# Sums of fetched activations formed on GpSimd, and two output banks copied by ScalarE, in a seven-product fp32 decoder trunk

## The reference

```python
for layer in range(2):
    mixer = fox_mixer if layer == 0 else retention_mixer
    h = h + mixer(rmsnorm(h, norm), ...)
    h = h + square(relu(rmsnorm(h, mlp_norm) @ w_up)) @ w_down    # 2048 -> 8192 -> 2048
return rmsnorm(h, final_norm)
```

## Time and profile before

| | us |
|---|---|
| median of 3 runs | 2564.88 (2563.68 to 2568.09) |
| the profiled execution | 2560.97 |
| its span, first to last instruction | 2559.2 |
| TensorE busy | 2489.9 (97%) |
| VectorE busy | 1962.1 (77%) |
| ScalarE busy | 1446.4 (57%) |
| GpSimd busy | 165.1 (6%) |

### The profile page before, as it was taken

One profiled execution on the slowest core, in us unless ns is written; L12 is line 12 of the kernel. 1 busy time (PEld: TensorE's weight loads), 2 busy tenths in 40 slices (PEclk: granted clock), 3 DMA queues, 4 the chain that ended last, 5 costly groups with the idle time before them and its releaser, 6 DMA issues. The chain is left out here.

```text
span 2559.2 us, 29454 instructions
## 1 busy us (share of the span) xinstructions
PE 2489.9 (97%) x11035; PEld 2045.9 (80%) x11035; DVE 1962.1 (77%) x2007; ACT 1446.4 (57%) x1694; POOL 165.1 (6%) x284
## 2 busy tenths in 40 slices
PE   9999999999999999989999999999999999999998
PEld 8888888788788787768888888888777887878876
DVE  6454556888787888867778867778888888788877
ACT  7454544656555656545556446556565556565654
POOL 0000000000100001101111001101100010010010
PEclk9999999999999999999999999999999999999999
DMA  8454556575757565756665666666576666657574
GB/s 311 150 176 149 172 174 226 189 256 193 231 182 259 187 244 196 248 168 206 214 220 184 233 187 216 199 201 224 206 247 217 221 213 202 228 194 258 179 237 163
DMA packets 133940, 534.79 MB, mean 209 GB/s; under 512 B 17200, under 2 KB 17456, under 8 KB 133424
## 3 DMA queue, kind: packets, MB, share of 16 engines
q1 hardware_dynamic: 115776, 476.65, 54.1%
q0 software_dynamic: 17888, 56.12, 7.3%
q10 hardware_dynamic: 144, 0.26, 0.0%
HBM read 506.74 MB, written 26.21 MB: 208 GB/s over the span
## 5 line engine op out<-in xcount | busy, mean ns | idle before, releaser
L1530 ACT ACTIVATE w_hi<-work 128x1024 fp32r<-128x1024 f32 (+2 forms) x847 | 960.6, 1154 | 718.8 <-DMA work<-in_w_wide 172.3
L2152 DVE TENSOR_TENSOR w_lo<-work,w_hi 128x1024 fp32r<-128x1024 f32 (+2 forms) x847 | 1117.0, 1348 | 323.8 <-ACT w_hi L1530 320.5
L1047 PE MATMUL acc<-w_hi,xT_hi 128*128 128x512 f32 x811 | 319.0, 393 | 7.9 <-DVE xT_lo L2218 3.9
L1049 PE MATMUL acc<-w_hi,xT_lo 128*128 128x512 f32 x811 | 317.4, 391 | 0.0
L1048 PE MATMUL acc<-w_lo,xT_hi 128*128 128x512 f32 x811 | 317.2, 391 | 0.0
L1047 PE MATMUL sc<-w_hi,xT_hi 128*128 128x512 f32 x676 | 264.1, 391 | 0.0
L1049 PE MATMUL sc<-w_hi,xT_lo 128*128 128x512 f32 x676 | 263.2, 389 | 0.0
L1048 PE MATMUL sc<-w_lo,xT_hi 128*128 128x512 f32 x676 | 263.0, 389 | 0.0
L1047 PE MATMUL acc<-w_hi,aT_hi 128*128 128x512 f32 x584 | 232.1, 397 | 11.2 <-DVE aT_lo L2218 5.5
L1915 DVE TENSOR_TENSOR w_lo<-work,w_hi 128x1024 fp32r<-128x1024 f32 x127 | 151.7, 1223 | 103.2 <-ACT w_hi L1322 100.9
L1048 PE MATMUL acc<-w_lo,aT_hi 128*128 128x512 f32 x584 | 229.3, 393 | 0.0
(11 more groups left out here) (321 smaller groups left out, 3887.6 us busy)
## 6 DMA issues: line engine op xcount, KB each, us to landing
work<-in_w_stream SPq DMA_DIRECT2D x400, 512.0 KB, 4.6
work<-in_w_wide SPq DMA_DIRECT2D x212, 768.0 KB, 6.6
work<-in_w_wide SPq DMA_DIRECT2D x178, 512.0 KB, 5.9
park<-stage POOLq DMA_DIRECT2D x38, 512.0 KB, 4.1
evac<-park POOLq DMA_DIRECT2D x152, 128.0 KB, 4.2
qk_park<-evac POOLq DMA_DIRECT2D x8, 512.0 KB, 6.0
work<-qk_park POOLq DMA_DIRECT2D x32, 128.0 KB, 5.4
h<-in_x SPq DMA_DIRECT2D x2, 1024.0 KB, 8.7
```

The costliest lines, as they stand in the source:

```text
L1047: pe.matmul(bank[:, :], x_hi, w_hi[:, c], start=start, stop=False, skip_group_check=True)
L1049: return pe.matmul(bank[:, :], x_lo, w_hi[:, c], start=False, stop=stop, skip_group_check=True)
L1530: ins = act.activation(w_hi[:, ring_cols(place, n)], src[:, first * NB:(first + n) * NB], ACT.Copy)
L2152: ins = dve.tensor_tensor(w_lo[:, c], src[:, first * NB:(first + n) * NB], w_hi[:, c].bitcast(F32), ALU.subtract)
```

## The change

1. VectorE's `wide_sums` and `turned_sums` are gone. GpSimd forms the sums in `turn`, behind the fetch of the turn that they need, with four `tensor_tensor` instructions and waits on its own semaphores; then it goes on to the next turn. There are 19 such groups: turns 0 and 1 of each of the eight chunks (256 and 128 columns), one group of 256 ahead of retention, and one of 256 and one of 128 ahead of the second MLP. The first MLP's very first sums are formed in another way, as before.
2. After a down pair that isn't followed by a norm (i = 3, 4, 7, 8, 11, 12 in each MLP) ScalarE copies banks e and w into the two `tr` banks (`copy_out`), ahead of `seed_u`, and VectorE adds the copies to `h` later, after `lo(7)` and `lo(8)` (`add_copy`).
3. After an up pair `seed_u` stands ahead of the square of the third relu.
4. In pair 15 ScalarE's first two squares of `h` move behind `hi(8)`, and VectorE's last `turn_lo` behind the add and the gain of its own banks. In retention's last output pair the second turn's `turn_hi` and `turn_lo` stand ahead of tile 16 instead of behind tile 17, and the split of the sums stands one tile earlier.

```diff
+            def turned_sums(n, count, first, j, sign):
+                w = width_of_sum(count)
...
+                pool.wait_ge(fetched, GRID * 16 * (n + 1))
+                wait(pool, s_lo, count - 1)
+                small_step(pool.tensor_tensor(s[S1], a21, a22, ALU.subtract))
+                if sign > 0:
+                    small_step(pool.tensor_tensor(s[S2], a11, s[S1], ALU.subtract))
+                else:
+                    small_step(pool.tensor_tensor(s[S2], s[S1], a11, ALU.subtract))
+                pool.tensor_tensor(s[S3], a11, a21, ALU.subtract)
+                pool.tensor_tensor(s[S4], a12, s[S2], ALU.subtract if sign > 0 else ALU.add).then_inc(s_made, 1)
+                pool.wait_ge(s_made, parts_of_sums(count - 1) + (2 if first else 1))
...
+                for m in range(2):
+                    chunk, quad = divmod(n - UPS_AT[m], QUADS)
+                    if 0 <= chunk < SUPER and quad < 2:
+                        turned_sums(n, UNITS[mlp_unit(m, 4 * chunk + 2)].sums, quad * 2 * P, 2 - quad, -1)
...
+            def copy_out(tok, done, bank, out, count, n):
+                act.wait_ge(done, count)
+                act.wait_ge(turned, n)
+                wait(act, copy_added[tok], T(f"copy{tok}"))
+                act.activation(tr[tok], bank[:, :], ACT.Copy).then_inc(out, 1)
+                T.up(f"copy{tok}")
...
@@ ScalarE, wide_pair
                 if was_up:
                     relu(0, e_done, sc[0], e_out, done, turn + 1)
                     relu(1, w_done, sc[1], w_out, done, turn + 1)
+                if copies:
+                    turns = UPS_AT[m] + (i + 1) // 4 * QUADS
+                    copy_out(0, e_done, sc[0], e_out, done, turns)
+                    copy_out(1, w_done, sc[1], w_out, done, turns)
+                seed_u(u, RET_HEADS * m)
+                if was_up:
                     relu_squared(0, e_out, done)
-                seed_u(u, RET_HEADS * m)
...
+            def add_copy(tok, quad, out, count):
+                dve.wait_ge(out, count)
+                dve.scalar_tensor_tensor(h_quad(tok, quad), tr[tok], inv_ms[:, tok:tok + 1], h_quad(tok, quad),
+                                         ALU.mult, ALU.add).then_inc(copy_added[tok], 1)
...
@@ VectorE, wide_pair
-                if not was_up:
+                if was_normed:
                     add_bank(0, p_quad + 1, sc[0], e_done, e_out, done, scaled=not by_pe)
...
                 lo(u, 7)
+                if copies:
+                    add_copy(0, p_quad + 1, e_out, done)
                 lo(u, 8)
+                if copies:
+                    add_copy(1, p_quad + 1, w_out, done)
                 if turn is not None and not late_norm:
-                    if new_sums:
-                        wide_sums(turn, 0)
                     turn_lo(turn, *dst, p_quad)
```

More of the change, by code:

```diff
@@ L152, in parts_of_sums, with width_of_sum @@
     return sum(1 if X_SUMS_OF_RET <= n < X_SUMS_OF_MLP else 2 for n in range(1, count + 1))
+def width_of_sum(count):
+    return (KT_SEVEN if X_SUMS_OF_RET <= count < X_SUMS_OF_MLP else KT_WIDE) // 2 * P
 def tiles_of(u):
@@ L599, in build_trunk @@
         full_out = sem("full_out")
+        copy_added = pair("copy_added")
+        sum_step = sem("sum_step")
         x_done, z_done, e_done, w_done = (sem(f"{n}_done") for n in ("x_bank", "z_bank", "e_bank", "w_bank"))
@@ L755, in _, with small_step @@
             load_gain(0)
+            def small_step(ins):
+                ins.then_inc(sum_step, 1)
+                small_steps[0] += 1
+                pool.wait_ge(sum_step, small_steps[0])
+            small_steps = [0]
+            def turned_sums(n, count, first, j, sign):
+                w = width_of_sum(count)
+                s = [mlp_sums[:, k * w + first:k * w + first + j * P].rearrange("p (j a r) -> p j a r", j=j, a=GRID)
+                     for k in range(4)]
+                (a11, a12), (a21, a22) = ([fetched_tiles[:, t, at:at + j] for at in (0, j)] for t in range(TOKS))
+                pool.wait_ge(fetched, GRID * 16 * (n + 1))
[8 more added lines that the diff above has]
+                pool.wait_ge(s_made, parts_of_sums(count - 1) + (2 if first else 1))
             def turn(n):
@@ L1307, in _ @@
         def _(act):
-            T = Tally("block", "tr0", "tr1", "squared", "group", "ret_head", "norm", "p5")
+            T = Tally("block", "tr0", "tr1", "squared", "group", "ret_head", "norm", "p5", "copy0", "copy1")
             def split(first, last, block0=False):
@@ L1705, in wo_pair @@
                     batch_hi(1, aT_hi, QUADS - 1)
-                for t in range(13, 18):
+                for t in range(13, 16):
                     hi(u, t)
@@ L1722, in wide_pair @@
                 new_sums = UNITS[u + 1].sums if i % 4 == 1 else 0
+                copies = not was_up and not was_normed
                 if by_pe:
@@ L1755, in wide_pair @@
                 hi(u, 8)
+                if late_norm:
+                    square_of_h(0, p_quad, x_out, done)
+                    square_of_h(1, p_quad, z_out, done)
                 if was_normed:
@@ L2411, in wo_pair @@
                 fold(1, quad + 1, g_sum, False)
+                if was_normed:
+                    turn_lo(MLP_NORM_AT + 1, xT_hi, xT_lo, 1)
                 lo(u, 16)
@@ L2414, in wo_pair @@
                 if was_normed:
-                    wide_sums(MLP_NORM_AT + 1, 1)
-                    turn_lo(MLP_NORM_AT + 1, xT_hi, xT_lo, 1)
+                    s_low(X_SUMS_OF_MLP)
                 add_bank(0, quad, acc[0], x_done, x_out, done + 1, scaled=False)
@@ L2503, in wide_pair @@
                     s_low(new_sums)
-                if turn is not None and late_norm:
-                    turn_lo(turn + 1, *dst, p_quad + 1)
                 if not up and u not in LATE:
@@ L2511, in wide_pair @@
                         wait_gain(dve, 1)
+                        dve.wait_ge(turned, turn + 2)
                         gained_after(0, quad, x_out, done + 1)
+                if turn is not None and late_norm:
+                    turn_lo(turn + 1, *dst, p_quad + 1)
             def rotated(hd, tok):
```

38 lines of the change are left out of this document (9 added, 29 removed).

## The result

| | before | after |
|---|---|---|
| median of 4 runs, us | 2564.28 (2562.52 to 2568.09) | 2589.77 (2585.92 to 2594.06) |
| the profiled execution, us | 2560.97 | 2589.35 |
| its span, us | 2559.2 | 2587.3 |
| mean granted TensorE clock | 0.990 | 0.985 |

The account below looks back on a forecast made before the run. One chain per chunk, from turn 1's transposes through DRAM to the seed, was taken to bound TensorE. 2.0 + 1.6 - 0.5 = +3.1 us a chunk, +24.8 for eight, -2.6 for copies: +22.2, so 2587 us; range 2557 to 2604.

Parts of the forecast that it names:

- Sums of turn 1: Behind turn 1's landing: GpSimd's four sums of 128 columns start `s_high` 3.95 instead of 2.35 us after it, +1.6 a chunk.
- the first rival: Sums stay beside the chain: those of turn 1 end within 2.35 us of the landing; -6.6 us, 2558 us; 18%.
- Sums of turn 0: Mid-pair: GpSimd's four sums of 256 columns stop VectorE 3.2 us, transposes of turn 1 up to 2.8 late; +2.0 a chunk.
- the last sentence: Of turn 0's term: a later write falls behind part of the weight loads, so only 2.0 of the 2.8 us pass on.
- The rival in which the DMA swallows the delay: Turn 1 lands when it did despite turn 0's late sums; only 1.6 - 0.5 a chunk remain, +6, 2571 us; 15%.
- Seed ahead of the square: Chain's end in each chunk: the seed starts at the square's earlier place, -0.5 us; the square, wanted much later, is covered.
- The copies: After down pairs: VectorE loses two adds ahead of `seed_w`, -2.6 us in all; ScalarE's two copies cost 0.
- The norms: Pair 15 and retention's last pair: both ends wait for TensorE itself, so 0, bounds -1.6 and +3.2 us.
- GpSimd is the one that waits: VectorE keeps GpSimd out: turn 0's sums run from `seed_w` on, S3 and S4 after `lo(last)`; +22, also 2587 us; 10%.
- Gains and losses cancel: Rival: sums of turn 0 free, those of turn 1 half a microsecond late; 2560 to 2570 us; 12%.
- What should show it: Seed waits beyond 30 us or new up-pair waits; VectorE 0.5 to 0.8 us longer; landing to `s_high` over 3; `seed_w` waits gone.

Follow-up runs that it names:

- sums_alone: Kernel before with only edit 1, all 19 groups of sums on GpSimd instead of VectorE: 2601.7 us, ratio 1.0139.
- sums_back: Changed kernel with all sums back on VectorE at their old places; copies, seed ahead of the square and moved turns stay: 2566.45 us, 1.0004 to before.
- turn0_alone: Kernel before with only the sums of 256 columns (turn 0 of each chunk, first turns of the norms) on GpSimd: 2585.65 us, ratio 1.0093.
- seed_down: Kernel before with the seed ahead of the square only in each chunk's first down pair: 2560.3 us, ratio 0.9983.
- turn1_alone: Kernel before with only the sums of 128 columns (turn 1) on GpSimd: 2580.22 us, ratio 1.0064.
- seed_up: Kernel before with the seed ahead of the square only in each chunk's second up pair: 2573.83 us, ratio 1.0035.

## Why the prediction was right, and where it wasn't

The time (2589.8 against 2587) and the direction came out as forecast, and by the mechanism forecast: GpSimd's sums on the chain of turn 1, shown by sums_alone and sums_back. But errors of opposite sign stand inside, and that the total is so near is in part luck.

- **Sums of turn 1, +1.6 a chunk.** 1.77, in all eight. The single pieces were off: 0.46 us for a sum where I took 0.55, and 0.08 us from one to the next where I took 0.5 from the earlier trace rows. Undisturbed, four would be over about 2.1 us after the landing, ahead of the 2.35 us that the first rival sets, and this term would have been 0. What decided was the taking of turns, S3 behind `turn_lo` and S4 behind `w_lo`. The forecast let S4 follow S3 without a gap; a `w_lo` between them was its bad end, priced +2.7. That order came, with shorter pieces, and that the two errors meet near 1.6 is luck. The trace shows that the stop works in both directions, which the prediction had no row for: the 1.51 us are GpSimd standing behind VectorE. The Trainium skill (SBUF — State Buffer, "Who interferes with whom") has the later one wait for a whole instruction, and these rows agree: VectorE, back to back, lets one GpSimd instruction in between two of its own.
- **Sums of turn 0, +2.0 of 2.8.** Two errors that cancel in part. The four sums held VectorE up by 2.2 us and not 3.2, so the delay ahead of the write was 1.8 us and not the 2.8 it could be. And the last sentence failed: the transfer swallowed none of it, its mean became 1.0 longer. The term read from the traces is +2.8, of which the 1.0 is little more than twice the uncertainty of such a mean. The rival in which the DMA swallows the delay is out: in turn0_alone, too, turn 1 lands 2.8 us later behind the read of turn 0, and 24 us are lost.
- **Seed ahead of the square, -0.5.** Right for the down pair (0.49; seed_down won 4.4 us). Missed: the diff moves it in the up pair too, where the seed waits for TensorE, and by itself that costs 9 us, more than the down pair wins. "The square is wanted much later; covered" looked at the down pair only, and at the square but not at the three `w_hi` behind it.
- **The copies, -2.6.** The wait went as worked out; the whole gain alone was 8 us, its interval from 4 to 13.
- **The norms, 0.** -0.17% by itself, 4.4 us (0.5 to 8.5), where the bound on this side was 1.6. With no row named for it, this term stays unexplained.
- **The clock, left out.** The sum counted waiting alone. In after, 12 of the 28 us are matmuls at the lower level. In turn0_alone and turn1_alone it is less, 6.0 and 2.7 us of TensorE's busy time, and the stretches already hold what falls before the seed's end.
- **Together:** 4.1 us a chunk instead of 3.1, and since the first chunk's first stretch hardly grew, 31.4 instead of 24.8 for eight. The seed's end is 25.1 us late in the last chunk and the program's end 28.1. The other 6.3 are won back between one chunk's seed and the next one's read of turn 0, half of them (868.65 us before, 865.48 after) in the stretch that holds retention.
- **The other rivals.** *GpSimd is the one that waits* is out for turn 0: its sums are over at 636.25, ahead of `seed_w` at 640.05, because VectorE lets one in after each of its own instructions. Behind the landing half of it holds, as S4 came only after `lo(last)`, but S3 did not. *Gains and losses cancel* is out: neither part of the sums is free.
- **What should show it** did in part: `s_high` more than 3 us behind the landing, VectorE's instructions 0.5 us longer, `w_lo` and `seed_e` waited for in the up pairs. The waits for `seed_w` in pairs 3, 7 and 11 are gone; the three left stand beside the norms. The waits for the seed did not grow beyond 30 us; they split, as TensorE now stops at `W_TAU1` too.

## What to carry to other kernels

Work moved from VectorE to GpSimd is priced by what VectorE does in the same microseconds, not by how long GpSimd takes alone: place it where VectorE's next deadline is far (the same sums cost 24 us ahead of the transposes and 5 behind them), never between a landing and the step that waits for it. When an instruction moves ahead of another in a shared piece of code, look at every place that runs this code: ahead of a consumer that waits it wins, and where the instruction itself must wait, all that is behind it in the queue pays. And when the longest wait ends in a chain with several late steps, look up the next one first: 6 us were taken off the seed, the step behind it gave way by only 1.4, and the whole gave nothing.

## What the runs showed of the hardware

- Where both had work, and VectorE's was subtractions and sums of two operands in SBUF, GpSimd and VectorE took turns, instruction by instruction. GpSimd's sums went from 0.46 to 1.51 us (128 columns) and up to 2.3 (256 columns, where undisturbed ones take 0.74). VectorE's `w_lo` of 1024 columns went from 1.23 to 1.49, `tau4` of 1536 from 1.75 to 2.30.
- The next GpSimd instruction behind a wait on its own semaphore starts 0.08 us after the one before has ended.
- A write and read through memory of 512 KB each took 15 to 20 us beside the weight loads, and up to 4 us apart within one execution. In seed_up, where a batch of loads goes out 0.3 to 0.5 us later, its mean is 2.1 us longer; that the one makes the other was not tried.
- Behind TensorE's waits of 4.15, 3.23 and 2.10 us the granted clock is at its lower level for 3 to 5 us, with matmuls of 0.63 us instead of 0.39. Behind others of 2.47 and 3.08 us it is not, so the length of the wait alone does not decide.
